# A two-block transformer kernel in fp32: gate and up of the second FFN by seven block products in place of eight

## The chip, the cores and the metric

One core of a Trainium2 chip (trn2) runs the whole program. The metric is device time in microseconds (us), median of several executions; lower is better.

## The reference, cut to what matters

Two layers are applied to 256 tokens of width 2048: a recurrent block with an FFN, then an attention block with an FFN. The change touches the second FFN alone:

```python
h2 = _rms(x, g_norm2) * (1 + sc2) + sh2          # 256 x 2048
gate, up = jnp.split(h2 @ w_ffn_in, 2, axis=-1)  # 2048 x 11264: gate | up, 5632 columns each
x = x + gt2 * ((jax.nn.silu(gate) * up) @ w_ffn_out)
```

All is float32. The kernel gets its precision from split products: each operand is a high part (rounded to float32r, the type of TensorE's fast pass) plus a low part (the rest, float32r too), and a product is high x high + low x high + high x low, three matmuls.

## The kernel before, in words

**Tiling.** Tokens are two blocks (tb) of 128. K = 2048 is 16 K-tiles of 128, in four groups (q) of 4. The FFN's 5632 columns are cut into 11 iterations of 512. In iteration i come gate (H times 512 columns), up (the same with the other half of the matrix), then the down product of the block of 512 hidden columns made one iteration earlier, over the four column blocks (n) of the output.

**Units and half-units.** Weights come in units of 1 MB (4 K-tiles x 512 columns), each a DMA that SP issues into one of four slots RAW0 to RAW3 (`load`, L363). `slot_free` makes SP wait until the unit four before is no longer read. A unit is two half-units (`sub`), each 2 K-tiles x 512 columns, 128x1024. For each, ScalarE writes the high part WHI (`hi`, L580), VectorE the low part WLO = RAW - WHI (`lo`, L1073), and TensorE multiplies (`sub` in the tensor block, kind "T", through `mm`, L1783): 2 K-tiles x 2 token blocks x 3 = 12 matmuls with 128 tokens stationary and 512 columns moving. An iteration has 24 half-units: 8 gate, 8 up, 8 down, 288 matmuls. Half-units are numbered through the whole program; the second FFN begins with number 552, its iteration 3 (the first that changes) with 616.

**Rings.** WHI and WLO have two places each, and in the FFNs a third (for the second FFN the three places are dealt out from half-unit 528 on, inside the output projection ahead of it). `ring(s)` gives a half-unit's place and how many half-units back the place was last used (deep); `hi` waits until TensorE is done with that one (semaphore `pe_sub`). Each engine works its queue strictly in order, and everything is ordered by semaphores: `hi_done` (ScalarE to VectorE), `lo_done` (VectorE to TensorE and SP), `free[pair]` (a PSUM pair is read out).

**PSUM.** The pairs A to D have two banks of 512 columns. Gate sums in A, up in B, down alternates between A and C. L724 (ScalarE) forms silu of A in G, L1302 (VectorE, `product`) multiplies by B, TensorE turns the result in 8 transposes (`hid_turn`, L2013), and L730 and L1307 write its high and low part, HID. `add_down(n)` (L1315, VectorE) adds a finished down block to YF and frees its pair; in the loop body it is placed behind low 20 and 22 for n = 0, 1, and behind low 0 and 2 of the next iteration for n = 2, 3.

**Modulation.** In the first three iterations VectorE also works on vectors of `w_ada_2`, which GpSimd loads (L514, 512 KB each, four slots); the last sum is `ada_bias` 24. Otherwise GpSimd computes nothing in this part. Just ahead of the FFN stands the boundary, where x is normalised and H formed (L1242 high part, L1243 low part).

**The loop.** Iterations 0 to 2 are written out, 3 to 8 are a loop on every engine, 9 and 10 are written out.

Of the kernel before, what the change touches and what calls it, by code (L numbers as in the profile page):

```python
# [22 lines left out]
T = 256  # L23
# [92 lines left out]
RING3 = ((2 * U_FFN1, 2 * U_WIN2 + 30), (2 * U_WOUT2 + 8, 2 * N_UNITS))  # L116


def ring(s):


    if s < 26:
        return s % 2, s
    for first, last in RING3:
        if first <= s < last:
            if s < first + 3:
                return (s - first) % 3, s - 47 if first == 2 * U_FFN1 else 2
            return (s - first) % 3, 3
    return s % 2, 2
# [25 lines left out]
class Counts:  # L155


    def __init__(self):
# [4 lines left out]
        self.quad, self.chain = Count(), Count()  # L163
        self.all = dict(unit=self.unit, sub=self.sub, A=self.A, B=self.B, C=self.C, ada=self.ada,
                        ada_group=self.ada_group, gate=self.gate, hid=self.hid, quad=self.quad, chain=self.chain)
# [25 lines left out]
def build(nc, x, c_rows, positions, rows_src, weights, ada_w, base_const, att_const, rg_a, rg_i, w_pool, out):  # L191
    w_in, w_out, w_gate, w_up, w_down, w_in2, w_uq, w_ukv, w_pa, w_pb, w_out2, w_ffin2, w_ffout2 = weights
    with ExitStack() as ctx:
# [18 lines left out]
        WLO2 = place("WLO2", [P, 2, COLS], F32R)  # L212
        here[0] = end
# [12 lines left out]
        WHI.append(WHI2)  # L226
        WLO.append(WLO2)
# [53 lines left out]
        chunk = lambda t, n: t[:, :, n * 512:(n + 1) * 512]  # L281
        row = lambda t, n: t[:, n * 512:(n + 1) * 512].rearrange("p (a b) -> p a b", a=1).to_broadcast([P, 2, 512])
# [10 lines left out]
        pe_tb = sem("pe_tb")  # L293
        free = {p: sem(f"free_{p}") for p in "ABC"}
# [52 lines left out]
        def _(sp):  # L347
            c = Counts()

            def slot_free():  # L350

                last = 2 * (c.unit.at - 4)
                if any(first <= last < end for first, end in NATIVE):
                    sp.wait_ge(pe_sub, last + 2)
                elif last >= 0:
# [23 lines left out]

            def ffn(k, wg, gcol, wu, ucol, wd):  # L380
# [7 lines left out]

                gate_up(0)
# [100 lines left out]

        def landed(eng, c):
# [7 lines left out]
        def _(pool):  # L499
# [56 lines left out]

            pool.wait_ge(free["B"], B_PROJ + 2)
            for g in (10, 11):
                ada(1, g * ADA_COLS)
# [3 lines left out]
        def _(act):  # L563
# [7 lines left out]
            def hi(n=1):  # L571

                for _ in range(n):
                    half, slot = c.sub.at % 2, c.unit.at % 4
# [142 lines left out]
            def ffn(k, skip, final=False):  # L717
# [15 lines left out]
                def body(skip=0, subs=24, previous=True, rows=False):  # L733
                    for s in range(skip, subs):
                        hi()
                        if s == 6 and previous:
# [5 lines left out]

                body(skip=skip, subs=16, previous=False)
                body()
                with act.Fori(2, NF - 2) as i:
                    c.enter(i - 2, unit=12, sub=24, hid=1, gate=1)
                    body()
                c.leave(NF - 4)
                body(rows=True)
# [309 lines left out]
        def _(dve):  # L1059
# [7 lines left out]
            def lo(n=1):  # L1067

                for _ in range(n):
                    half, slot = c.sub.at % 2, c.unit.at % 4  # L1070
# [1314 lines left out]
```

## Time and profile before

| | |
|---|---|
| time, median of 3 runs | 2519.57 us (2518.47 to 2519.95) |
| profiled execution: span from first to last instruction | 2517.7 us |
| profiled execution: time outside its span | not listed; the span is 1.9 us under the median of the runs |
| TensorE busy | 2440.5 us, 97% |
| VectorE busy | 1793.1 us, 71% |
| ScalarE busy | 1082.6 us, 43% |
| GpSimd busy | 223.2 us, 9% |
| DMA | 643 MB, mean 255 GB/s |

Busy time says how long an engine had an instruction running; matmuls overlap in the records, so TensorE's busy time is no measure of its peak. PE is TensorE, DVE VectorE, ACT ScalarE, POOL GpSimd, SP the engine that issues the weights' DMAs. "Idle before" is an engine's idle time just ahead of an instruction, with what ended it.

### The profile page before, as it was taken

What the parts mean: (1) busy time and instruction counts of PE and PEld (TensorE: products, weight loads), DVE (VectorE), ACT (ScalarE), POOL (GpSimd) and SP (SyncE); (2) the same over time, 40 slices, a digit from 0 to 9 for tenths busy, and PEclk for the clock granted to TensorE, in tenths of its full rate; (3) what the DMA queues carried; (4) which work ended last, traced back from release to release, by engine and by line L of the source; (5) the groups of instructions that cost most, each with busy time, mean ns of one, the idle gap of its engine ahead of it and who ended that gap; (6) DMA issues with size and microseconds to landing.
All of it is one profiled execution on the core that took longest, in us unless ns stands there. A gap on an engine that the chain in (4) does not pass through costs nothing.

```text
span 2517.7 us, 30560 instructions
## 1 busy us (share of the span) xinstructions
PE 2440.5 (97%) x11620; PEld 2000.9 (79%) x11620; DVE 1793.1 (71%) x1751; ACT 1082.6 (43%) x1243; POOL 223.2 (9%) x397
## 2 busy tenths in 40 slices
PE   4899999999999999999999999999999999999999
PEld 3679448888888888879997778788788888888887
DVE  6878887888888888778785445865688555555565
ACT  2035124444444444464346557644544444444443
POOL 4412210111111111001110000000011000000000
PEclk8899999999999999999999999999999999999999
DMA  9999996898889888647985555355588555555654
GB/s 367 382 337 354 403 358 225 308 328 313 312 321 328 317 318 323 209 152 279 341 291 162 166 172 161 117 184 200 198 320 285 191 192 185 197 184 192 208 184 150
DMA packets 291262, 643.01 MB, mean 255 GB/s; under 512 B 21883, under 2 KB 34749, under 8 KB 290269
## 3 DMA queue, kind: packets, MB, share of 16 engines
q1 hardware_dynamic: 234512, 436.45, 50.8%
q0 software_dynamic: 56096, 205.02, 21.8%
q8 instruction: 68, 1.11, 0.2%
q10 hardware_dynamic: 556, 0.18, 0.0%
q14 instruction: 30, 0.24, 0.0%
HBM read 639.47 MB, written 2.13 MB: 255 GB/s over the span
## 4 chain that ended last, share of the span: by engine, by line
PE 86%; DVE 5%; DMA 4%; ACT 4%; issue 1%; POOL 0%; DVEq 0%; ACTq 0%; POOLq 0%
PE PS L1783 84%; DMA R<-in_w_ada 3%; DVE R L1093 2%; ACT WHI L580 1%; DVE WLO L1073 1%; DMA RAW<-in_w_ffn_gate 1%; PE PS L2013 1%; PE PS L1907 1%; PE PS L1938 0%; DVE H L1243 0%; ACT R L658 0%; ACT L945 0%; ACT L588 0%; DVE H L1242 0%; ACT L937 0%
## 5 line engine op out<-in xcount | busy, mean ns | idle before, releaser
L1073 DVE TENSOR_TENSOR WLO<-RAW,WHI 128x1024 fp32r<-128x1024 f32 x760 | 929.7, 1225 | 610.3 <-ACT WHI L580 608.0
L580 ACT ACTIVATE WHI<-RAW 128x1024 fp32r<-128x1024 f32 x760 | 805.5, 1061 | 1118.3 <-PE PS L1783 1103.0
L1783 PE MATMUL PS<-WHI,H 128*128 128x512 f32 x4064 | 1263.1, 392 | 5.7 <-DVE WLO L1073 5.0
L1783 PEld LDWEIGHTS PS<-WHI,H 128*128 128x128 f32 x4064 | 755.0, 188 | 173.8 <-DVE WLO L1073 16.0
L1783 PE MATMUL PS<-WLO,H 128*128 128x512 f32 x2032 | 792.1, 390 | 0.0
L1783 PEld LDWEIGHTS PS<-WLO,H 128*128 128x128 f32 x2032 | 381.4, 188 | 80.8
L1093 DVE SCALAR_TENSOR_TENSOR R<-R,CA 128x1024 f32<-128x1024 f32 x326 | 417.6, 1281 | 36.7 <-DMA R<-in_w_ada 29.7
L1783 PE MATMUL PS<-WHI,HID 128*128 128x512 f32 x1280 | 395.2, 390 | 0.0
L514 POOL DMA_DIRECT2D R<-in_w_ada x284 | 150.9, 531 | 1586.7 <-DVE R L1090 555.1
L1783 PEld LDWEIGHTS PS<-WHI,HID 128*128 128x128 f32 x1280 | 239.3, 188 | 49.0
L1783 PE MATMUL PS<-WLO,HID 128*128 128x512 f32 x640 | 249.1, 389 | 0.0
L1783 PE MATMUL PS<-H,WHI 128*128 128x256 f32 x1120 | 204.8, 285 | 3.1 <-DVE WLO L1073 3.1
L1783 PEld LDWEIGHTS PS<-H,WHI 128*128 128x128 f32 x1120 | 174.7, 192 | 5.6 <-DVE WLO L1073 5.2
L1783 PE MATMUL PS<-H,WLO 128*128 128x256 f32 x560 | 158.4, 283 | 0.0
L1783 PEld LDWEIGHTS PS<-WLO,HID 128*128 128x128 f32 x640 | 120.1, 188 | 25.0
L1783 PE MATMUL PS<-RAW,YF 128*128 128x512 f32 x256 | 110.8, 592 | 0.0
L1783 PEld LDWEIGHTS PS<-H,WLO 128*128 128x128 f32 x560 | 107.3, 192 | 0.0
L1783 PEld LDWEIGHTS PS<-RAW,YF 128*128 128x128 f32 x256 | 48.2, 190 | 58.7 <-issue 58.7
L1315 DVE TENSOR_TENSOR YF<-PS,YF 128x1024 f32<-128x1024 f32 x72 | 87.7, 1218 | 0.0
L1783 PE MATMUL PS<-R,RAW 128*128 128x256 f32 x256 | 65.9, 425 | 13.3 <-ACT R L658 13.3
L1783 PEld LDWEIGHTS PS<-R,RAW 128*128 128x128 f32 x256 | 55.1, 217 | 22.8 <-ACT R L658 13.7
L1783 PE MATMUL PS<-R 128*128 128x256 f32 (+1 forms) x250 | 49.7, 341 | 3.7 <-ACT R L1031 1.8
(233 smaller groups left out, 1233.7 us busy)
## 6 DMA issues: line engine op xcount, KB each, us to landing
R<-in_w_ada POOLq DMA_DIRECT2D x348, 512.0 KB, 6.7
RAW<-in_w_in SPq DMA_DIRECT2D x88, 1024.0 KB, 5.6
RAW<-in_w_ffn_in SPq DMA_DIRECT2D x88, 1024.0 KB, 5.0
RAW<-in_w_ffn_gate SPq DMA_DIRECT2D x44, 1024.0 KB, 6.9
RAW<-in_w_ffn_up SPq DMA_DIRECT2D x44, 1024.0 KB, 5.3
RAW<-in_w_ffn_down SPq DMA_DIRECT2D x44, 1024.0 KB, 8.3
RAW<-in_w_ffn_out SPq DMA_DIRECT2D x44, 1024.0 KB, 5.0
RAW<-in_w_out SPq DMA_DIRECT2D x32, 1024.0 KB, 7.3
```

The lines of the kernel that those rows point to most:

```text
L514: pool.dma_start(ADA[slot], ada_w[layer][:, k, bass.ds(col, ADA_COLS)])\
L580: nc.scalar.activation(WHI[j][:, :, :], RAW[slot][:, 2 * half:2 * half + 2, :], ACT.Copy)\
L1073: nc.vector.tensor_tensor(WLO[j][:, :, :], RAW[slot][:, 2 * half:2 * half + 2, :], WHI[j][:, :, :].bitcast(F32), ALU.subtract).then_inc(lo ...
L1093: ins = nc.vector.scalar_tensor_tensor(acc, ADA[slot], scalar, acc, ALU.mult, ALU.add)
L1315: nc.vector.tensor_tensor(chunk(yt, n), PAIR[pair][:, :, :], chunk(yt, n), ALU.add)\
L1783: return nc.tensor.matmul(o, a, b, start=start, stop=stop, skip_group_check=True)
L1907: ins = nc.tensor.transpose(flat("D")[:, j * P:(j + 1) * P], acc[:, j * P:(j + 1) * P], ident)
L2013: ins = nc.tensor.transpose(four("B")[:, t, tb * P:(tb + 1) * P], G[:, tb * 512 + t * P:tb * 512 + (t + 1) * P], ident)
```

## The change

The second FFN's iterations 3 to 9 are called turns 0 to 6 and written out. In each, for the K-tile groups q = 0 and 1 (NS = 2), gate and up are taken together as one product of 2 x 2 blocks: the rows are the two token blocks, the columns gate and up, the inner index the two halves of the group (2 K-tiles each). Eight block products become seven, by sums and differences of blocks on both sides. Each of the seven pieces is a half-unit of its own with a WHI and a WLO, but only 6 matmuls (2 K-tiles x 3). Groups 2 and 3 keep their eight products, `both_halves`, 12 matmuls each. A turn has 30 half-units: 14 pieces (0 to 13), 4 gate (14 to 17), 4 up (18 to 21), 8 down (22 to 29).

- **Sums of weights**: four per group, 128x1024, on GpSimd (`column_sums`), in five places USUM in free parts of R.
- **Lows on GpSimd**: half-units 17, 21, 23 and 25 of each turn have their low part made by GpSimd (`low_here`); VectorE skips them.
- **Sums of H**: once, during iteration 0, GpSimd forms four combinations of H's blocks per group (`operand_sums`: one pass of 128x1024, four of 128x256) and their low parts (`operand_low`); ScalarE writes the high parts behind half-units 13 and 15 of iteration 0.
- **Ring**: four places in the turns, three again afterwards (`place_of`).
- **PSUM**: each pair's banks hold one of seven sums; ScalarE copies the shared first product (Q1_COPY), VectorE puts gate and up together in eight additions of 128x512 (`seven_ev`).
- **Hidden block**: turned in two halves (`half_turn`), each 128x512 for ScalarE and VectorE; `product` of iteration 2 comes forward to its half-unit 18.
- **Slots**: SP also waits for GpSimd's lows (`lo_pool`) and sums (`u_done`); order of a turn's loads: gate and up of group 0, of group 1, gate 2 and 3, up 2 and 3, four down.

```diff
-RING3 = ((2 * U_FFN1, 2 * U_WIN2 + 30), (2 * U_WOUT2 + 8, 2 * N_UNITS))
+NS = 2
+SEVEN_FIRST, SEVEN_LAST = 3, NF - 1
+U_SEVEN = U_FFN2 + 8 + 12 * 2
+SUB_SEVEN = 2 * U_SEVEN
+PER_SEVEN = 24 + 3 * NS
+GATE_END = 7 * NS + 2 * (4 - NS)
+UP_END = GATE_END + 2 * (4 - NS)
+POOL_LOW = (GATE_END - 1, UP_END - 1, UP_END + 1, UP_END + 3)
...
+def place_of(s):
+
+    if s < SUB_SEVEN:
+        return (s - RING3[1][0]) % 3
+    return (s - SUB_SEVEN) % 4 if s < SUB_AFTER else (s - SUB_AFTER) % 3
...
+    if s >= SUB_SEVEN:
+        before = [n for n in range(max(s - 8, RING3[1][0]), s) if place_of(n) == place_of(s)]
+        return place_of(s), s - before[-1] if before else 0
...
+            def column_sums(turn, q):
+
+                unit, first = U_SEVEN + 12 * turn + 2 * q, 4 * (NS * turn + q)
+                g, u = RAW[unit % 4], RAW[(unit + 1) % 4]
+                of = lambda n: USUM[(first + n) % 5]
+
+                def place_free(n):
+                    if first + n >= 5:
+                        t, m = divmod(first + n - 5, 4 * NS)
+                        sub = SUB_SEVEN + PER_SEVEN * t + m // 4 * 7 + 3 + m % 4
+                        pool.wait_ge(lo_done, dve_lows(sub + 1))
+                    else:
+                        pool.wait_ge(a_lo, NS)
+                        if first + n >= 2:
+                            pool.wait_ge(ada_bias, 24)
+
+                landed_unit(pool, unit)
+                landed_unit(pool, unit + 1)
+                place_free(0)
+                pool.tensor_tensor(of(0), g[:, 0:2, :], u[:, 0:2, :], ALU.add).then_inc(u_done, 1)
+                place_free(1)
+                pool.wait_ge(u_done, first + 1)
+                pool.tensor_tensor(of(1), of(0), u[:, 2:4, :], ALU.add).then_inc(u_done, 1)
+                place_free(2)
+                pool.tensor_tensor(of(2), u[:, 0:2, :], u[:, 2:4, :], ALU.add).then_inc(u_done, 1)
+                place_free(3)
+                pool.wait_ge(u_done, first + 2)
+                pool.tensor_tensor(of(3), of(1), g[:, 2:4, :], ALU.add).then_inc(u_done, 1)
...
+                        operand_low(NS - 1)
+            for turn in range(N_SEVEN):
+                for q in range(NS):
+                    column_sums(turn, q)
+                for at in POOL_LOW:
+                    unit, half = divmod(at - 7 * NS, 2)
+                    low_here(SUB_SEVEN + PER_SEVEN * turn + at, U_SEVEN + 12 * turn + 2 * NS + unit, half)
 
...
+                def high(src, ready, value):
...
+                    if deep:
+                        act.wait_ge(pe_sub, c.sub.value(1 - deep))
+                    else:
+                        act.wait_ge(ada_bias, 24)
+                    nc.scalar.activation(WHI[j][:, :, :], src, ACT.Copy).then_inc(hi_done, 1)
...
+                            if at == 11:
+                                act.wait_ge(half_t, turn + 1)
+                                nc.scalar.activation(HID[:, 0:2, 0:T], MISC.rearrange("p (a b) -> p a b", a=2), ACT.Copy)\
+                                    .then_inc(half_hi, 1)
+                            if at == 16:
+                                act.wait_ge(hid_t, c.hid.value(1))
+                                nc.scalar.activation(HID[:, 2:4, 0:T], MISC.rearrange("p (a b) -> p a b", a=2), ACT.Copy)\
+                                    .then_inc(hid_hi, 1)
+                                c.hid.at += 1
+                            if at == 7 * (NS - 1) + 4:
+                                act.wait_ge(pe_sub, first + 7 * (NS - 1) + 1)
+                                if turn:
+                                    act.wait_ge(seven_ev, 8 * turn)
+                                else:
+                                    act.wait_ge(a_lo, NS)
+                                nc.scalar.activation(Q1_COPY, bank("A", 0), ACT.Copy).then_inc(q1_copied, 1)
+                            if at == GATE_END + 5:
+                                act.wait_ge(seven_ev, 8 * turn + 6)
+                                nc.scalar.activation(G, G, ACT.Silu).then_inc(gate_done, 1)
+                                c.gate.at += 1
...
+                            if at in (1, 3):
+                                add_down(2 + at // 2, 4)
+                            if at == 11:
+                                dve.wait_ge(half_hi, turn + 1)
+                                nc.vector.tensor_tensor(HID[:, 0:2, T:2 * T], half, HID[:, 0:2, 0:T].bitcast(F32),
+                                                        ALU.subtract).then_inc(half_lo, 1)
+                            if at == 16:
+                                dve.wait_ge(hid_hi, c.hid.value(1))
+                                nc.vector.tensor_tensor(HID[:, 2:4, T:2 * T], half, HID[:, 2:4, 0:T].bitcast(F32),
+                                                        ALU.subtract).then_inc(hid_lo, 1)
+                                c.hid.at += 1
+                            if at == 7 * NS + 1:
+                                dve.wait_ge(q1_copied, turn + 1)
+                                dve.wait_ge(pe_sub, first + last + 5)
+                                if turn == 0:
+                                    dve.wait_ge(a_lo, NS)
+                                nc.vector.tensor_tensor(vy_sum, bank("C", 0), Q1_COPY, ALU.subtract).then_inc(seven_ev, 1)
+                            if at == 7 * NS + 2:
+                                dve.wait_ge(pe_sub, first + last + 6)
+                                dve.wait_ge(seven_ev, 8 * turn + 1)
+                                nc.vector.tensor_tensor(X_SUM, bank("C", 1), vy_sum, ALU.add).then_inc(seven_ev, 1)
+                                nc.vector.tensor_tensor(w_sum, bank("B", 1), vy_sum, ALU.add).then_inc(seven_ev, 1)
+                                dve.wait_ge(seven_ev, 8 * turn + 3)
+                                nc.vector.tensor_tensor(vy_sum, bank("B", 1), X_SUM, ALU.add).then_inc(seven_ev, 1)
+                            if at == GATE_END + 3:
+                                dve.wait_ge(pe_sub, first + GATE_END)
...
+                                nc.vector.tensor_tensor(silu[:, 0, :], bank("A", 1), Q1_COPY, ALU.add).then_inc(seven_ev, 1)
+                                nc.vector.tensor_tensor(silu[:, 1, :], bank("D", 0), X_SUM, ALU.subtract).then_inc(seven_ev, 1)
+                            if at == UP_END + 3:
+                                dve.wait_ge(pe_sub, first + UP_END)
+                                dve.wait_ge(seven_ev, 8 * turn + 4)
+                                nc.vector.tensor_tensor(w_sum, bank("B", 0), w_sum, ALU.add).then_inc(seven_ev, 1)
+                                nc.vector.tensor_tensor(vy_sum, bank("D", 1), vy_sum, ALU.add).then_inc(seven_ev, 1)
+                            if at == UP_END + 4:
+                                dve.wait_ge(gate_done, c.hid.value(1))
+                                dve.wait_ge(seven_ev, 8 * turn + 8)
+                                nc.vector.tensor_tensor(G, WY_SUM, G, ALU.mult).then_inc(up_done, 1)
+                            if at in (UP_END + 5, UP_END + 7):
+                                add_down((at - UP_END - 5) // 2, 4)
...
+                def piece(out_, high, low, first, last):
+
+                    j, _ = ring(c.sub.at)
+                    low_ready()
+                    for k in range(2):
+                        mm(out_, high(k), WHI[j][:, k, :], first and k == 0)
+                        mm(out_, low(k), WHI[j][:, k, :], False)
+                        ins = mm(out_, high(k), WLO[j][:, k, :], False, last and k == 1)
+                    ins.then_inc(pe_sub, 1)
+                    c.sub.at += 1
...
+                def by_sevens(turn):
+
+                    ev = 8 * (turn - 1)
+                    if turn == 0:
+                        pe.wait_ge(a_lo, NS)
+                    for q in range(NS):
+                        first, last = q == 0, q == NS - 1
+                        plain = lambda at, tb: [lambda k, x=x: H[:, at + k, x + tb * P:x + (tb + 1) * P] for x in (0, T)]
+                        mixed = lambda m: [lambda k, of=of: of[q][:, m, k, :] for of in (AHI, ALO)]
+                        if first:
+                            pe.wait_ge(free["A"], c.A.value())
+                        piece(bank("A", 0), *plain(4 * q, 0), first, last)
+                        piece(bank("A", 1), *plain(4 * q + 2, 0), first, False)
+                        if first:
+                            if turn:
+                                pe.wait_ge(seven_ev, ev + 7)
+                            else:
+                                pe.wait_ge(up_done, c.hid.value(1))
+                        piece(bank("B", 0), *mixed(3), first, False)
+                        piece(bank("B", 1), *mixed(0), first, last)
+                        if q == 0 and turn == 0:
+                            row_turn(k, gate_at, 24)
+                        if first:
+                            pe.wait_ge(free["C"], c.C.value())
+                        piece(bank("C", 0), *mixed(1), first, last)
+                        if q == 1:
+                            pe.wait_ge(half_lo, turn + 1)
+                            half_turn(1)
+                        piece(bank("C", 1), *mixed(2), first, last)
+                        if first:
+                            if turn:
+                                pe.wait_ge(seven_ev, ev + 6)
+                            else:
+                                pe.wait_ge(ada_bias, 24)
+                        piece(bank("D", 0), *plain(4 * q + 2, 1), first, False)
+                        if q == 0:
+                            if turn:
+                                pe.wait_ge(seven_ev, ev + 8)
+                            else:
+                                pe.wait_ge(row_ev, k + 1)
+                            pe.wait_ge(up_done, c.hid.value(1))
+                            half_turn(0)
+                    for q in range(NS, 4):
+                        for half in range(2):
+                            both_halves(bank("A", 1), bank("D", 0), 4 * q + 2 * half, False, q == 3 and half == 1)
+                    pe.wait_ge(hid_lo, c.hid.value(1))
+                    for q in range(NS, 4):
+                        for half in range(2):
+                            both_halves(bank("B", 0), bank("D", 1), 4 * q + 2 * half, q == NS and half == 0,
+                                        q == 3 and half == 1)
+                    c.gate.at += 1
+                    pe.wait_ge(q1_copied, turn + 1)
+                    pe.wait_ge(seven_ev, 8 * turn + 5)
+                    for n in range(4):
+                        group("AC"[n % 2], kind="T", src=HID, units=1)
+                    c.hid.at += 1
+
                 previous = {3: hid_turn}
                 gate(turned=(k, "DC"))
```

## Rows read from the trace of the kernel before

**Rows 1.** Page, part 1: busy us (share of span), instructions.

```profile
PE 2440.5 (97%) x11620; PEld 2000.9 (79%) x11620; DVE 1793.1 (71%) x1751; ACT 1082.6 (43%) x1243; POOL 223.2 (9%) x397
```

**Rows 2.** Chain that ended last, second FFN: start us, us, what.

```profile
2039.40 65.31 PE PS L1783 x288
2104.70 0.87 PE PS L2013 x8
2105.58 65.33 PE PS L1783 x288
...
2171.78 65.30 PE PS L1783 x288
```

**Rows 3.** Busy time by stretch, the seven iterations: busy us (instructions).

```profile
1961.40:2027.60 66.20, 66.20 (x298) 54.88 (x297) 36.22 (x31) 27.29 (x26) 0.00 (x0) 1.00 0.57 191
1961.40:2424.80 463.40, 463.40 (x2075) 384.09 (x2074) 253.52 (x211) 191.20 (x183) 0.00 (x0) 1.00 0.58 193
```

**Rows 4.** Who waited for whom, 1961.4 to 2424.8 us: total, times, longest.

```profile
ACT WHI L580 <- PE PS L1783: 260.7, 161, 2.0
DVE WLO L1073 <- ACT WHI L580: 209.9, 168, 2.4
```

**Rows 5.** Groups by line, 2000 to 2400 us: busy, mean ns, idle before.

```profile
L1073 DVE TENSOR_TENSOR WLO<-RAW,WHI 128x1024 fp32r<-128x1024 f32 x146 | 179.0, 1226 | 182.9 <-ACT WHI L580 182.9
L1315 DVE TENSOR_TENSOR YF<-PS,YF 128x1024 f32<-128x1024 f32 x24 | 29.2, 1218 | 0.0
...
L580 ACT ACTIVATE WHI<-RAW 128x1024 fp32r<-128x1024 f32 x145 | 153.8, 1061 | 225.2 <-PE PS L1783 225.2
...
L730 ACT ACTIVATE HID<-PS 128x1024 fp32r<-128x1024 f32 x6 | 6.1, 1010 | 0.0
```

**Rows 6.** Timeline of VectorE: start us, us of one or several (xcount).

```profile
1774.60 0.69 DVE L1189 TENSOR_TENSOR R<-PS,R 128x512 f32<-128x512 f32 x1
...
1798.10 2.35 DVE L1073 TENSOR_TENSOR WLO<-RAW,WHI 128x1024 fp32r<-128x1024 f32 x2
...
2161.15 1.23 DVE L1073 TENSOR_TENSOR WLO<-RAW,WHI 128x1024 fp32r<-128x1024 f32 x1 [0.36 <-ACT WHI L580]
2162.30 1.22 DVE L1315 TENSOR_TENSOR YF<-PS,YF 128x1024 f32<-128x1024 f32 x1
```

**Rows 7.** Timeline around one hand-over: TensorE, ScalarE, VectorE.

```profile
2167.79 0.39 PE L1783 MATMUL PS<-WLO,H 128*128 128x512 f32 x1
...
2168.22 1.06 ACT L580 ACTIVATE WHI<-RAW 128x1024 fp32r<-128x1024 f32 x1 [1.66 <-PE PS L1783]
...
2169.31 1.23 DVE L1073 TENSOR_TENSOR WLO<-RAW,WHI 128x1024 fp32r<-128x1024 f32 x1 [1.49 <-ACT WHI L580]
```

**Rows 8.** DMA issues, 1990 to 2440 us: size, median us to landing.

```profile
RAW<-in_w_ffn_in SPq DMA_DIRECT2D x55, 1024.0 KB, 5.0
RAW<-in_w_ffn_out SPq DMA_DIRECT2D x27, 1024.0 KB, 5.0
```

**Rows 9.** Timeline of GpSimd and VectorE, 114 to 117 us.

```profile
114.75 1.82 POOL L537 MEMSET R<- 128x2048 f32 x1
...
114.58 1.28 DVE L1093 SCALAR_TENSOR_TENSOR R<-R,CA 128x1024 f32<-128x1024 f32 x1 [0.83 <-DMA R<-in_w_ada]
116.70 1.28 DVE L1093 SCALAR_TENSOR_TENSOR R<-R,CA 128x1024 f32<-128x1024 f32 x1 [0.83 <-DMA R<-in_w_ada]
```

**Rows 10.** Timeline at the start of the second FFN, VectorE and GpSimd.

```profile
1797.49 0.69 DVE L1243 TENSOR_TENSOR H<-R,H 128x512 fp32r<-128x512 f32 x1
...
1775.58 2.15 POOL L514 DMA_DIRECT2D R<-in_w_ada  x4 [472.61 <-DVE R L1189]
1833.27 0.53 POOL L514 DMA_DIRECT2D R<-in_w_ada  x1 [55.54 <-DVE R L1090]
```

More of the change, by code:

```diff
@@ L489, in build, with landed_unit, seven_source @@
         EXTRA = {U_KPE: 1, **{U_LAT + n: 3 for n in range(7)}}
+        def landed_unit(eng, n):
+            extra = sum(v for u, v in EXTRA.items() if u % 4 == n % 4 and u <= n)
+            eng.wait_ge(raw_in[n % 4], 16 * (n // 4 + 1 + extra))
+        def seven_source(turn, q, e):
+            unit = U_SEVEN + 12 * turn + 2 * q
+            g, u = RAW[unit % 4], RAW[(unit + 1) % 4]
+            return (g[:, 0:2, :], g[:, 2:4, :], u[:, 2:4, :])[e] if e < 3 else USUM[(4 * (NS * turn + q) + e - 3) % 5]
         def landed(eng, c):
@@ L557, in _, with low_here @@
+            def low_here(sub, unit, half):
+                j, _ = ring(sub)
+                pool.wait_ge(hi_done, sub + 1 - native_before(sub))
+                pool.tensor_tensor(WLO[j][:, :, :], RAW[unit % 4][:, 2 * half:2 * half + 2, :],
+                                   WHI[j][:, :, :].bitcast(F32), ALU.subtract).then_inc(lo_pool, 1)
             pool.wait_ge(free["B"], B_PROJ + 2)
             for g in (10, 11):
-                ada(1, g * ADA_COLS)
+                for k in range(KT):
+                    pool.wait_ge(ada_op, c.ada.value(-3))
+                    pool.dma_start(ADA[c.ada.at % 4], ada_w[1][:, k, g * ADA_COLS:(g + 1) * ADA_COLS])\
+                        .then_inc(ada_in[c.ada.at % 4], 16)
+                    c.ada.at += 1
+                    if g == 10 and k == 3:
+                        pool.wait_ge(x_step, 12)
+                        for q in range(NS):
+                            operand_sums(q)
+                            if q:
+                                operand_low(q - 1)
+                        operand_low(NS - 1)
@@ L1350, in body @@
                             lo()
+                        if s == 18 and early:
+                            product(3)
                         if s == 1 and up:
@@ new lines, in half_turn, with both_halves @@
+                def half_turn(n):
+                    for t in (2 * n, 2 * n + 1):
+                        for tb in range(2):
+                            ins = nc.tensor.transpose(MISC[:, t % 2 * T + tb * P:t % 2 * T + (tb + 1) * P],
+                                                      G[:, tb * 512 + t * P:tb * 512 + (t + 1) * P], ident)
+                    ins.then_inc(hid_t if n else half_t, 1)
+                def both_halves(one, two, at, first, last):
+                    j, _ = ring(c.sub.at)
+                    low_ready()
+                    for k in range(2):
+                        for tb, out_ in ((0, one), (1, two)):
+                            high, low = (H[:, at + k, x + tb * P:x + (tb + 1) * P] for x in (0, T))
+                            mm(out_, high, WHI[j][:, k, :], first and tb == 1 and k == 0)
+                            mm(out_, low, WHI[j][:, k, :], False)
+                            ins = mm(out_, high, WLO[j][:, k, :], False, last and k == 1)
+                    ins.then_inc(pe_sub, 1)
+                    c.sub.at += 1
@@ L2307, in _ @@
             ffn(3, False, mod_at(1, 5))
[L2308 removed]
+            assert c.sub.at == N_SUBS
 def kernel(**inputs):
```

234 lines of the change are left out of this document (202 added, 32 removed).

## The prediction

> **What bounds the kernel now.** I read the page's shares first, then the chain that ended last, then the stretch that the change rewrites, then single instructions. TensorE is busy 97% of the span; VectorE, the next, 71%, and GpSimd 9% [rows 1]. In the second FFN the chain is TensorE alone: 288 matmuls in 65.3 us, then the 8 transposes of the hidden block in 0.87 us, over and over [rows 2]. So an iteration takes 66.2 us and one 128x512 matmul 65.31 / 288 = 0.2268 us of the stream (the 390 ns of its row overlap with the next). The seven iterations that change run from 1961.4 to 2424.8 us: 463.4 us, TensorE 100% busy at a granted clock of 1.00 (the 2.4 GHz level), VectorE busy 253.5 us (55%), ScalarE 191, GpSimd 0, the DMA engines 0.58 [rows 3]. ScalarE and VectorE mostly wait for TensorE to give back a ring place [rows 4]. Only fewer matmuls shorten this stretch, and only if the operands still come in time.
>
> **What goes.** Gate and up of one group of four K-tiles are 4 half-units of 12 matmuls, 48. By sevens they are 7 pieces of 6, 42. Two groups save 12 matmuls an iteration: 12 x 0.2268 = 2.72 us, in seven iterations 19.05 us. The columns, types and transposes stay. All of it lies on the chain.
>
> **What the pieces ask of the other engines.** 14 pieces of 6 x 0.2268 = 1.361 us make a window of 19.05 us per iteration. Each piece needs its own high part on ScalarE (1.06 us) and low part on VectorE (1.23 us) [rows 5]; back to back VectorE starts one every 1.13 to 1.15 us, and an addition out of PSUM takes the same 1.15 [rows 6]. In the window VectorE has 14 lows (16.1 us), two additions of the down product (2.3) and half a hidden block (0.6, from 0.69 for 128x512 [rows 6]): 19.0 of 19.05 us. ScalarE has 14 x 1.06 and two copies of half width, 15.9. It fits, with nothing to spare. What carries it is the ring, now four deep: TensorE's half-unit ends at 2168.18, the high part starts 2168.22, the low starts 2169.31 and ends 2170.54 [rows 7], a round of 2.4 us (2.56 from the start of TensorE's next piece, since its last matmul ends 0.16 us into it); TensorE comes to that place three pieces, 4.08 us, later. Slack 1.5 us; an addition of 1.15 goes into it. I take no stall here. Outside the window VectorE has 12 lows, nine passes of half width out of PSUM, two additions and a product, some 23 us in 44.4: covered. The other waits (the halves of the hidden block, the copied first product, the bank sums) each sit one to three pieces behind their producers, where the ring has them ready; I cost them at nothing, and they are due next if VectorE falls back. The loop is written out; its back edges cost nothing measurable now (65.30 to 65.33 us each time [rows 2]), so this is zero too.
>
> **The two joints.** Here I find a cost. The old ring has three places, counted from another start: half-unit 615 lies in place (615-528) mod 3 = 0, and the first piece, 616, is given place 0 as well. Its high part must wait until the half-unit just before it is multiplied. Behind it stand in VectorE's queue low 0, low 1 and the addition that frees pair A, for which the first piece waits. So TensorE stands for 0.16 + 2.4 + 1.15 + 1.15 = 4.9 us, once. The pieces after that find VectorE 1.15 us per low against 1.361: no more. On leaving, the first half-unit is only two deep and again waits for low 0 and one addition: 0.16 + 2.4 + 1.15 - 2.72 = 1.0 us. Together 5.9 us.
>
> **DMA and slots.** The bytes are the same, 12 units of 1 MB per iteration, 5.0 us from issue to landing [rows 8]. Slots of the two groups are freed by GpSimd's sums now. The up unit of the first group is loaded when low 25 is done, some 18 us before the window, and lands 12 us before it; that of the second follows low 29 and lands about 3 us before it. SP only waits at its own slots. Nothing lost.
>
> **GpSimd, the unknown.** Per iteration it gets 8 column sums and 4 lows of 128x1024, 12 passes, and no row shows it doing arithmetic on two inputs. The nearest is a memset of 128x2048 in 1.82 us [rows 9]: 0.91 us for 1024 elements of one stream, the lower bound; three streams (two read, one written) one after the other give 2.73, the upper. Two reads one after the other with the write hidden give 1.8. I take 2.3, the middle of 1.8 and 2.73. By a row of the Trainium skill ("GPSIMD Engine Reference", 3.1) an fp32 tensor_tensor of 2048 elements takes 4497 ns, thus an estimate of 2.25 here; no run here shows it, and the sum would not change. In time: eight sums at 2.3 need 18.4 us from 12 us before the window, so they end some 6 us into it, and the last is wanted at 14.5. At 2.73 it is 10: still in time. So GpSimd's own speed does not bind; what it does to VectorE may. Bounds for that: nothing (the VectorE pass with two SBUF inputs that began 0.17 us ahead of the memset kept its 1.28 us, and the memset ran beside it [rows 9], though a memset only writes), and full exclusion, rival one. I take nothing to slight, because the nearest row shows none. A gain is excluded: nothing gets shorter from a second user.
>
> **Before the first turn** GpSimd forms the mixed operands of H: ten passes and two lows, at most 18 us, after H is finished at 1798.2. Its queue has the next load of w_ada behind them, which goes out at 1833.3 [rows 10]: 17 us to spare. ScalarE's two copies stand behind half-units 13 and 15, where it idles 1.66 us ahead of each high part [rows 7]. Nothing.
>
> **Sum.** -19.05 + 5.9 = -13.15 us, on a span of 2517.7 us, which stands 1.9 us under the median of 2519.57; I subtract from the median: 2506.4 us.
>
> **Rivals.**
> One, **VectorE and GpSimd exclude each other**: a VectorE pass with two SBUF inputs (every low) and a GpSimd pass that reads SBUF cannot run together. The four sums of the second group fall into the window, as its unit lands 3 us ahead of it. Then lows and sums share one path: 16.1 + 4p against 19.05 + 1.5 of slack, a stall of 4p - 4.45; with p = 2.3, 4.75 us, against 2.72 saved. That is +2.03 x 7 = 14.2, with the joints +20.1: 2539.7 us, slower. It decides from p = 1.6 on (a stall of 1.9 leaves 0.84 us a turn, and seven of those pay the joints); p = 1.8 gives 2525.7, p = 2.73 2552. For it: VectorE's window is full, so whatever GpSimd takes is added. Against: no row of before shows it, and rows 9 show none for a write. The Trainium skill ("SBUF — State Buffer", Who interferes with whom) states just such a rule, that a Vector instruction with two SBUF inputs contends with a GpSimd instruction that reads SBUF and that the second one fully blocks; nothing in this trace can show or deny it for a read. By that rule the time is this rival's.
> Two, **a mild mutual slowing**: lows overlapping a sum are stretched. Up to some 1.5 us per window goes into the slack; at 3 us, 1.5 us a turn is lost: 7 x (1.5 - 2.72) + 5.9 = -2.6, 2517 us, no change.
> Three, **the joints are covered** after all: -19.05, 2500.5 us, if the first piece does not wait as I read it.
>
> **How the numbers follow.** The forecast (no or slight interference) 0.50, with its own range of 2500 to 2512; full exclusion 0.36; the middle case 0.12, spread over all three signs; something else 0.02. A difference of about 0.2%, 5 us, is what a measurement here can tell from none. Faster 0.54, same 0.07, slower 0.39. The range reaches from the joints nearly covered (2502) to exclusion at slightly over my p (2541); about 2 in 10 stay out, most of it above.
>
> **What would show it.** Right: TensorE's busy runs in the seven turns sum to 63.5 us each, one gap of about 5 us near 1961 us, low rows of VectorE unchanged at 1.23 us, GpSimd passes near 2.3 us. Wrong: lows of 2 us and more, or gaps ahead of them, wherever a GpSimd pass runs; TensorE waiting for VectorE's lows around pieces 4, 11 and 12 of every turn; or GpSimd passes above 3 us, with ScalarE waiting for a sum.

## The result, and the profile after

The changed kernel takes 2553.2 us (median; 2552.23 to 2554.75), the kernel before 2519.57: ratio 1.0133, with a 95% interval of 1.0119 to 1.0148. It is slower by 33.6 us; I had forecast 13 us less. The profiled execution has a span of 2552.1 us, 34.4 more than before. Executions of one kernel agree within 0.5% here; one of the four of experiment 5 took 6018.29 us and is left out of its time. The page's first part, to hold against [rows 1]:

```profile
PE 2432.2 (95%) x11536; PEld 1982.8 (78%) x11536; DVE 1931.9 (76%) x1828; ACT 1130.1 (44%) x1301; POOL 483.5 (19%) x493
```

The 84 matmuls are gone (11620 to 11536). TensorE's busy time falls by 8.3 us only, not by 19: beside a stop the records of two matmuls no longer overlap, and behind the first stop the matmuls are slower. VectorE has 138.8 us more busy time for 77 more instructions, GpSimd 260 us more. Next the chain that ended last, where [rows 2] had TensorE alone; one turn, from one transpose of the half block to the next, and the way out of the seven turns (start us, us, what):

```profile
2130.09 0.44 PE PS L2399 x4
2130.53 32.69 PE PS L2123 x144
2163.30 1.07 ACT WHI L949
2164.39 6.17 DVE WLO L1622 x2
2170.56 1.14 DVE YF L1585
2171.70 5.54 DVE WLO L1622 x2
2177.24 1.14 DVE YF L1585
2178.37 3.33 DVE WLO L1622 x2
2181.70 1.13 DVE YF L1585
2182.84 10.24 DVE WLO L1622 x4
2193.12 7.10 PE PS L2123 x30
2200.22 0.44 PE PS L2399 x4
...
2457.65 1.15 DVE YF L1585
2458.93 11.13 PE PS L2123 x48
```

From 2164.4 to 2193.1 the chain is VectorE: ten lows in 25.28 us and three additions in 3.41. The additions, which read PSUM, keep the 1.15 us of before; a low goes at 2.5 us instead of 1.15. The same pattern stands six times, at each passage from one turn to the next; the first turn has a stop of its own. The turn takes 2200.22 - 2130.09 = 70.1 us, 66.2 before [rows 2]. The stretches (PE, PEld, DVE, ACT, POOL busy with instructions; granted clock, DMA share, GB/s), against [rows 3]:

```profile
1961.90:1982.70 20.80, 12.42 (x48) 9.50 (x47) 18.63 (x11) 11.47 (x12) 12.77 (x5) 0.84 0.29 102
2122.97:2193.12 70.15, 64.89 (x284) 52.30 (x284) 56.01 (x42) 33.89 (x34) 34.26 (x12) 1.00 0.53 180
```

The first row is the way into the turns, at a mean granted clock of 0.84. In a turn (second row) TensorE's records cover 64.89 of 70.15 us. The clock is full, so this is waiting. The groups by line and shape, 2100 to 2400 us (busy, mean ns, idle before), against [rows 5]:

```profile
L1622 DVE TENSOR_TENSOR WLO<-RAW,WHI 128x1024 fp32r<-128x1024 f32 x76 | 139.3, 1854 | 53.7 <-ACT WHI L949 53.7
...
L1622 DVE TENSOR_TENSOR WLO<-R,WHI 128x1024 fp32r<-128x1024 f32 x36 | 59.8, 1699 | 0.0
...
L739 POOL TENSOR_TENSOR WLO<-RAW,WHI 128x1024 fp32r<-128x1024 f32 x16 | 38.4, 2402 | 108.7 <-ACT WHI L949 108.7
...
L733 POOL TENSOR_TENSOR R<-R,RAW 128x1024 f32<-128x1024 f32 x10 | 33.7, 3374 | 0.0
...
L1585 DVE TENSOR_TENSOR YF<-PS,YF 128x1024 f32<-128x1024 f32 x19 | 23.0, 1213 | 0.0
```

VectorE's low goes from 1226 ns to 1854 (and 1699 for those that read a sum). The same kind of pass on GpSimd takes 2402 ns where it stands beside no low of VectorE (L739) and 2760 to 3374 in the four sums (L733 is the last). L1585 is unchanged at 1213 against 1218. Where the long ones lie, the timelines of the same turn say; VectorE first, then GpSimd:

```profile
2164.39 6.17 DVE L1622 TENSOR_TENSOR WLO<-RAW,WHI 128x1024 fp32r<-128x1024 f32 x2 [0.42 <-ACT WHI L949]
2170.49 1.21 DVE L1585 TENSOR_TENSOR YF<-PS,YF 128x1024 f32<-128x1024 f32 x1
...
2195.26 2.35 DVE L1622 TENSOR_TENSOR WLO<-R,WHI 128x1024 fp32r<-128x1024 f32 x2
```

```profile
2163.74 2.40 POOL L725 TENSOR_TENSOR R<-RAW,RAW 128x1024 f32<-128x1024 f32 x1 [5.13 <-issue]
...
2169.44 3.36 POOL L730 TENSOR_TENSOR R<-RAW 128x1024 f32<-128x1024 f32 x1
...
2188.62 3.37 POOL L733 TENSOR_TENSOR R<-R,RAW 128x1024 f32<-128x1024 f32 x1
2204.72 2.40 POOL L739 TENSOR_TENSOR WLO<-RAW,WHI 128x1024 fp32r<-128x1024 f32 x1 [12.73 <-ACT WHI L949]
```

The first slow pair of lows begins 0.65 us after the first sum; once the eighth sum has ended at 2191.99 a pair takes 2.35 us again. GpSimd's 3.36 us is about one pass of its own (2.40, of which some hides) and one low (1.13). Both fit engines that wait for each other's whole pass, turn about. An addition from PSUM at 2170.49 lies beside the sum of 2169.44 and keeps its 1.21 us.

**Where 34.4 us come from**, by the starts of matmuls in TensorE's timeline (the next one would begin 0.23 us after the last). The matmul after iteration 2 would have begun at about 1961.75 (1961.27 before). The first piece begins at 1968.88: 7.1 us. The first matmul behind the seven turns would have begun at 2457.80 and begins at 2458.93: 1.1 us. Between lie 488.9 us; the turns without a wait are 63.53 us each (measured in the second experiment), 444.7, so 44.2 us are waits and lower clock inside the turns: 40.2 in the six passages, the rest in the first turn. Saved are 7 x (66.20 - 63.53) = 18.7. Sum: 0.5 + 7.1 + 1.1 + 44.2 - 18.7 = 34.2.

### The profile page after: what moved, and what is told of

The parts are those of the page before. It is cut to its first block, busy times and chain, and to the rows that moved or that the text cites. A ratio compares the mean times of both kernels' runs of the same rounds, so it can differ in the third digit from the quotient of the medians.

```text
span 2552.1 us, 30121 instructions
## 1 busy us (share of the span) xinstructions
PE 2432.2 (95%) x11536; PEld 1982.8 (78%) x11536; DVE 1931.9 (76%) x1828; ACT 1130.1 (44%) x1301; POOL 483.5 (19%) x493
## 4 chain that ended last, share of the span: by engine, by line
PE 76%; DVE 13%; DMA 5%; ACT 3%; issue 1%; POOL 0%; DVEq 0%; ACTq 0%; POOLq 0%
PE PS L2123 74%; DVE WLO L1622 6%; DMA R<-in_w_ada 5%; DVE R L1363 2%; ACT WHI L782 1%; DVE WLO L1343 1%; DVE YF L1585 1%; DMA RAW<-in_w_ffn_gate 1%; PE PS L2257 1%; PE PS L2363 1%; PE PS L2288 0%; ACT WHI L949 0%; DVE H L1513 0%; ACT L1215 0%; ACT L790 0%
## 5 line engine op out<-in xcount | busy, mean ns | idle before, releaser
L2123 PE MATMUL PS<-WHI,H 128*128 128x512 f32 x3784 | 1180.1, 393 | 37.1 <-DVE WLO L1622 17.0
L1343 DVE TENSOR_TENSOR WLO<-RAW,WHI 128x1024 fp32r<-128x1024 f32 x592 | 730.8, 1237 | 395.5 <-ACT WHI L782 393.1
L782 ACT ACTIVATE WHI<-RAW 128x1024 fp32r<-128x1024 f32 x592 | 627.2, 1061 | 862.5 <-PE PS L2123 845.1
L2123 PEld LDWEIGHTS PS<-WHI,H 128*128 128x128 f32 x3784 | 702.2, 188 | 201.4 <-issue 24.9
L2123 PE MATMUL PS<-WLO,H 128*128 128x512 f32 x1892 | 738.3, 390 | 0.0
L2123 PEld LDWEIGHTS PS<-WLO,H 128*128 128x128 f32 x1892 | 355.5, 188 | 75.8
L1622 DVE TENSOR_TENSOR WLO<-RAW,WHI 128x1024 fp32r<-128x1024 f32 x126 | 217.7, 1749 | 100.1 <-ACT WHI L949 100.1
L949 ACT ACTIVATE WHI<-RAW 128x1024 fp32r<-128x1024 f32 x154 | 163.1, 1061 | 199.5 <-PE PS L2123 199.5
L739 POOL TENSOR_TENSOR WLO<-RAW,WHI 128x1024 fp32r<-128x1024 f32 x28 | 67.3, 2403 | 190.1 <-ACT WHI L949 190.1
```

What stands on the lines that cost most here:

```text
L739: pool.tensor_tensor(WLO[j][:, :, :], RAW[unit % 4][:, 2 * half:2 * half + 2, :], WHI[j][:, :, :].bitcast(F32), ALU.subtract).then_inc(lo_ ...
L782: nc.scalar.activation(WHI[j][:, :, :], RAW[slot][:, 2 * half:2 * half + 2, :], ACT.Copy)\
L949: nc.scalar.activation(WHI[j][:, :, :], src, ACT.Copy).then_inc(hi_done, 1)
L1343: nc.vector.tensor_tensor(WLO[j][:, :, :], RAW[slot][:, 2 * half:2 * half + 2, :], WHI[j][:, :, :].bitcast(F32), ALU.subtract).then_inc(lo ...
L1622: nc.vector.tensor_tensor(WLO[j][:, :, :], src, WHI[j][:, :, :].bitcast(F32), ALU.subtract)\
L2123: return nc.tensor.matmul(o, a, b, start=start, stop=stop, skip_group_check=True)
```

## The experiments

Theory A in the expectations is mutual exclusion, the prediction's first rival: VectorE passes with both inputs in SBUF and GpSimd passes that read SBUF run one at a time. Its rivals are named where they stand. In experiments 1 to 4 the kernel before took 2520.83 us (2518.43 to 2522.83), in 5 to 8 2519.23 (2517.79 to 2521.65); ratios are against those.

**1. The joints alone.** The ring places of the turns are counted one further, so that the first piece does not share its place with the half-unit just before it; the wait on leaving the turns goes with the same edit.

```diff
-    return (s - SUB_SEVEN) % 4 if s < SUB_AFTER else (s - SUB_AFTER) % 3
+    return (s - SUB_SEVEN + 1) % 4 if s < SUB_AFTER else (s - SUB_AFTER) % 3
```

> The changed kernel with the ring's places shifted by one in the turns, so that the first piece and the half-unit before it do not share a place; nothing else. Theory A (VectorE passes with two SBUF inputs and GpSimd passes that read SBUF exclude each other): the one wait of about 7 us ahead of the first piece and the 1 us wait on leaving go, but turn 0 then shows the same 6.7 us of waits as the others; each turn stays at 70.1 us; 2546 us (2543 to 2549). Rival B (the joints are the main cost, since a stop of 7 us also lowers TensorE's granted clock): below 2535 us.

Measured: 2551.38 us (2551.15 to 2554.35), ratio 1.0125 [1.0108, 1.0142]; span 2549.7. The later turns still take 70.1 us (the half turn's transposes start at 2059 and 2129). The first turn's 7.1 us stop has shrunk to 2.4 us (again with a lower clock behind it) and the one on leaving is gone, but the first turn now has stops like the others', as its chain shows:

```profile
1964.55 5.49 DVE WLO L1622 x2
1971.17 10.24 DVE WLO L1622 x4
1981.45 7.10 PE PS L2123 x30
```

So the joints are 2.4 us of the span and no more while the sums are there: in the first turn the same queue of lows stood behind. The time lies above the expected range of 2543 to 2549 us: I had taken the whole stop for gone, and 2.4 us of it stayed. Rival B is out: the loss is not the joints'.

**2. No sums.** Pieces 3 to 6 of each group take raw blocks in place of the sums, GpSimd has no lows, and slots are freed after the group's last low. The eight sums per turn are left out; the matmuls, highs and lows are all there (the lows all on VectorE).

```diff
-POOL_LOW = (GATE_END - 1, UP_END - 1, UP_END + 1, UP_END + 3)
+POOL_LOW = ()
...
-            return (g[:, 0:2, :], g[:, 2:4, :], u[:, 2:4, :])[e] if e < 3 else USUM[(4 * (NS * turn + q) + e - 3) % 5]
+            return (g[:, 0:2, :], g[:, 2:4, :], u[:, 2:4, :], g[:, 0:2, :], g[:, 2:4, :], u[:, 0:2, :],
+                    u[:, 2:4, :])[e]
...
-                for q in range(NS):
-                    column_sums(turn, q)
```

> The changed kernel without GpSimd in the turns: the eight column sums are left out (pieces 3 to 6 take blocks of the raw weights in their place) and the four lows go back to VectorE. Left out: the sums of weights. Theory A: every low is back at 1.23 us, turns take 63.5 us, only the joints are left: 2507 us (2505 to 2510). Rival C (VectorE and ScalarE have too much to do for pieces of 1.36 us, GpSimd or not): turns stay above 66.2 us, 2520 us or more.

Measured: 2510.09 us (2509.67 to 2511.11), at the upper edge of the expected range; ratio 0.9961 [0.9946, 0.9975]; span 2507.8. The chain at the joint and in a turn, a group by line (2000 to 2400 us), and two stretches:

```profile
1962.62 2.36 DVE WLO L1619 x2
...
1966.22 8.03 PE PS L2120 x24
...
1985.78 0.44 PE PS L2396 x4
1986.21 55.81 PE PS L2120 x246
```

```profile
L1619 DVE TENSOR_TENSOR WLO<-RAW,WHI 128x1024 fp32r<-128x1024 f32 x187 | 225.3, 1223 | 101.6 <-ACT WHI L946 100.0
```

```profile
1966.22:1974.25 8.03, 8.03 (x26) 6.31 (x27) 5.99 (x6) 3.19 (x3) 0.00 (x0) 0.69 0.00 0
1985.78:2049.30 63.52, 63.52 (x286) 52.60 (x285) 47.68 (x46) 33.92 (x34) 0.00 (x0) 1.00 0.58 199
```

Every wait inside the turns is gone, with more work on VectorE than in the changed kernel (30 lows a turn, not 26). A turn is 63.52 us: the window's 19.0 us of VectorE in 19.05 does fit, and so do the ring, the halves of the hidden block and the slots. The first joint costs its stop, 4.9 us by the starts of matmuls (4.78 idle), and then lower clock: 24 matmuls take 8.03 us at a mean granted clock of 0.69, against 5.73 us at full clock in experiment 5. On leaving, the stop is 1.1 us.

**3. Writes only.** Each sum becomes three memsets of the same size at the same place in GpSimd's queue, with the same waits and signals; GpSimd has no lows. The sums' values are left out. The cut shows the first of the four sums of a group; the others are changed alike.

```diff
-                pool.tensor_tensor(of(0), g[:, 0:2, :], u[:, 0:2, :], ALU.add).then_inc(u_done, 1)
+                step(pool.memset(of(0), 0.0))
+                step(pool.memset(of(0), 0.5))
+                pool.memset(of(0), 0.25).then_inc(u_done, 1)
```

> As the run without GpSimd lows, but each column sum is replaced by three memsets of the same place (some 2.8 us together, no SBUF read), with the same waits and signals. Left out: the sums of weights, constants stand in their places. Theory A (only a GpSimd pass that reads SBUF excludes VectorE): lows stay at 1.23 us and turns at 63.5 us, 2507 us (2505 to 2512). Rival D (GpSimd's sums come too late, whatever VectorE does): turns about as long as with the sums, over 2540 us. Rival E (any GpSimd pass, writes too, takes the port): lows of 2 us and more, over 2535 us.

Measured: 2510.51 us (2509.38 to 2512.78), ratio 0.9962 [0.9947, 0.9976]. GpSimd and VectorE in one window:

```profile
2163.01 0.96 POOL L730 MEMSET R<- 128x1024 f32 x1 [1.75 <-DVE WLO L1630]
2164.02 0.96 POOL L731 MEMSET R<- 128x1024 f32 x1
```

```profile
2164.00 3.49 DVE L1630 TENSOR_TENSOR WLO<-R,WHI 128x1024 fp32r<-128x1024 f32 x3
```

GpSimd is busy nearly as long (2.9 us for a sum), writes three times the bytes, and the waits of its sums remain; three lows take 3.49 us, as without it, and a turn is 63.52 us, 22.7 of them with GpSimd busy. So neither GpSimd's writes, nor the waits for its sums, nor the freeing of slots by them cost anything. What costs is what a sum has and a memset lacks: it reads two inputs from SBUF. (It also adds, which this run does not part from the reading.) This is also why [rows 9] misled me: they show a memset.

**4. No lows on GpSimd**, the sums kept: only `POOL_LOW = ()`.

> The changed kernel with the four lows of a turn back on VectorE, the eight sums still on GpSimd. Theory A: the four lows lie outside the stretch where TensorE waits, and low 25, which frees the slot of the first group's up unit, takes 1.1 us in place of 2.4; so the sums begin about 1.3 us earlier and at most that is won per turn: 2548 us (2543 to 2554). Rival C (VectorE is overloaded): four more passes of 1.13 us a turn, 2565 to 2585 us.

Measured: 2547.68 us (2546.05 to 2549.34), ratio 1.0107 [1.009, 1.0124]; the turn 69.2 us. VectorE takes on four lows a turn and the span is 6.0 us shorter (2546.1 against 2552.1): a low moved to GpSimd was no relief. The loss stays with the sums; their groups read 2938, 2805, 3352 and 3382 ns, about as in the changed kernel. The last of them, 2000 to 2400 us:

```profile
L733 POOL TENSOR_TENSOR R<-R,RAW 128x1024 f32<-128x1024 f32 x12 | 40.6, 3382 | 0.0
```

This run and experiment 3 differ in nothing but the passes that stand for the sums, additions here and memsets there: 2547.68 against 2510.51 us, a turn of 69.2 against 63.5. It is the pair that isolates the cause.

**5. Neither sums nor the joint**: experiment 2 with the edit of 1.

> As the run without sums, with the ring's places shifted so that neither joint shares a place. Left out: the sums of weights. Theory A: nothing but the saved matmuls remains: 2501 us (2499 to 2504), 9 us below the run without sums, of which some 5.9 us is the waiting itself and the rest the lower granted clock after it. Rival: the joints are cheap when nothing else is late: 2507 us or more.

Measured: 2503.39 us (2500.63 to 2503.71, three executions), ratio 0.9932 [0.9912, 0.9952]; span 2501.6.

```profile
1962.73 0.87 issue
1963.60 5.73 PE PS L2120 x24
```

Against experiment 2 that is 6.2 us of span for the two joints alone. The stop falls to 0.87 us, the one on leaving is gone, and the next 24 matmuls take 5.73 us instead of 8.03, at full clock. This is about the floor of the scheme as it is ordered here.

**6. The sums on VectorE.** The whole computation; all sums but the first four of the first turn move into VectorE's queue, after half-units 1, 3, 6, 10 (second group) and 27 to 29 and 0 (next turn's first group); no lows on GpSimd; the joint as in 1.

```diff
+                SUM_AFTER = (1, 3, 6, 10)
+                NEXT_AFTER = (27, 28, 29, 30)
...
+                    nc.vector.tensor_tensor(of(n), a, b, ALU.add).then_inc(u_dve, 1)
```

> The computation of the changed kernel, complete, with the column sums and all lows on VectorE (sums of the next turn's first group behind lows 27, 28, 29 and 0, those of the second behind lows 1, 3, 6 and 10) and the joints mended. GpSimd only makes the first four sums. Theory A: no exclusion any more, a sum costs 1.15 us and not 2.4; the window now holds 16.1 + 5.7 + 2.9 us of VectorE's work in 19.05 us, so some 1.5 to 2 us of waiting per turn against 2.72 saved: 2512 us (2507 to 2518). Rival C (VectorE cannot carry it): 2525 us or more.

Measured: 2515.8 us (2513.06 to 2521.53), ratio 0.999 [0.9981, 1.0], hardly told apart from the kernel before; span 2512.6. Chain, and one group of 2000 to 2400 us:

```profile
1960.16 5.61 issue
1965.78 8.09 PE PS L2161 x24
```

```profile
L1656 DVE TENSOR_TENSOR R<-R,RAW 128x1024 f32<-128x1024 f32 x24 | 29.3, 1220 | 0.2
```

VectorE does in 1.22 us what GpSimd did in 2.4 to 3.4, and from the first piece on no low is longer than 1.23. The turn falls from 70.1 us (69.2 in experiment 4, which also has every low on VectorE) to 64.6, though VectorE has all 30 lows and all eight sums. What is left is the full window, as counted (1.1 us a turn), and a stop of 5.6 us in the first turn. That stop is this run's own: VectorE's first sum waits, idle for 2.33 us, until GpSimd has ended the fourth of the sums left to it, and the addition that frees pair A stands behind.

**7. The sums on VectorE, the two groups apart.** As 6 (the cut is against 6), but the turn's order is group 0's pieces, the four gate half-units of groups 2 and 3, group 1's pieces, the rest; loads, slots and waits follow.

```diff
+ORDER = [*range(7), *range(14, 18), *range(7, 14), *range(18, 30)]
...
-                SUM_AFTER = (1, 3, 6, 10)
+                SUM_AFTER = (7, 8, 9, 10)
```

> As the run with sums on VectorE, and the turn is reordered: the seven pieces of group 0, the four gate half-units of groups 2 and 3, the seven pieces of group 1, then up and down; the sums of group 1 lie behind the four gate half-units. VectorE then has 10.4 us in 9.5, 9.2 in 10.9, 8.7 in 9.5, 9.4 in 10.9 and 18.6 in 21.8. Theory A: every stretch fits, turns of 63.5 us: 2501 us (2499 to 2506). Rival C: over 2510 us.

Measured: 2506.19 us (2504.99 to 2509.79), at the upper edge of the expected range; ratio 0.9947 [0.9931, 0.9964]: faster than both kernels, by 13 us than the one before and some 47 than the changed one. Its turns have no wait; VectorE is busy 56.0 us in 63.5:

```profile
1966.21 2.03 issue
1968.24 7.29 PE PS L2168 x24
...
1991.58 51.73 PE PS L2168 x228
2043.31 0.44 PE PS L2444 x4
```

```profile
1991.58:2055.10 63.52, 63.52 (x285) 52.58 (x285) 56.01 (x53) 34.15 (x35) 0.00 (x0) 1.00 0.57 197
```

It keeps one stop of 2.03 us in the first turn and the lower clock after it (7.29 us for 24 matmuls). The profiled execution is the slowest of the four.

**8. The same order, the sums on GpSimd.** The rival to 6 and 7 was that the order alone gives the gain, since the sums then fall where VectorE has room. This run has the order, loads and slots of 7, with all eight sums on GpSimd as in experiment 4.

> The same reordered turn with the eight sums back on GpSimd, lows on VectorE. Theory A: in a turn 30 lows of 1.14 and 8 sums of 2.4 exclude each other, 53.4 us of 63.5, so it can fit on the whole, but four sums that alternate with lows need some 13 us, more than the 10.9 us of the gate half-units: some waiting ahead of the pieces of group 1, none ahead of group 0; 2510 us (2502 to 2525). Rival F (how the work is spread is all that matters, not which engine sums): as the reordered turn with sums on VectorE, 2501 us.

Measured: 2522.57 us (2514.29 to 2525.02), ratio 1.001 [1.0, 1.0019], again hardly told apart from the kernel before; the turn 66.5 us. The groups, 2000 to 2400 us, of this run:

```profile
L1628 DVE TENSOR_TENSOR WLO<-RAW,WHI 128x1024 fp32r<-128x1024 f32 x133 | 241.9, 1843 | 30.1 <-ACT WHI L954 28.1
L1628 DVE TENSOR_TENSOR WLO<-R,WHI 128x1024 fp32r<-128x1024 f32 x48 | 58.0, 1221 | 3.6 <-ACT WHI L954 3.1
```

The lows of pieces 3 to 6, which no longer lie beside a sum, are back at 1221 ns, the others stand at 1843 in the mean. TensorE waits most where the four gate half-units are, whose lows alternate with sums (four lows in 13.2 us), but also 0.8 us ahead of group 0, where I had expected nothing. The order helps, as a turn falls from 69.2 us (experiment 4) to 66.5, but the engine matters as much: from 66.5 to 63.5 with the sums on VectorE, 16 us of the median in all. So rival F is out, and GpSimd as a helper is worse here than no helper.

## Why the prediction was wrong

**What bounds the kernel, and what goes: right.** TensorE's stream bounds it, and a turn without waits is 63.52 us. The saving is 18.7 us, against 19.05 by my terms.

**The window: right, and no help.** I had VectorE at 19.0 of 19.05 us and the ring with 1.5 us of slack, and took no stall. Experiment 2 has exactly that load and no stall. But a window that is full to the last half microsecond turns every microsecond taken from VectorE into one of TensorE's, and I said so only in the rival's part.

**The joints: the stops right, the clock left out.** I had 4.9 + 1.0 us. Without the sums the stops measured 4.9 and 1.1 (experiment 2); what I left out is the 2.3 us that the lower clock cost after the first (24 matmuls in 8.03 us, not 5.73). With the sums the first stop was 7.1 us, as two lows in it took 4.55 us in place of 2.36. In the changed kernel itself the joints were worth only 2.4 us (experiment 1), since other waits stood behind them.

**DMA and slots: right.** Waiting for the signals of GpSimd's sums costs nothing (experiment 3).

**GpSimd's own speed: right.** I took 2.3 us for a pass; alone it takes 2.40. The estimate from the Trainium skill's figure ("GPSIMD Engine Reference", 3.1), halved to 2.25, stands 0.15 under it.

**GpSimd beside VectorE: the step that failed.** "I take nothing to slight, because the nearest row shows none." The row [rows 9] was a write beside a pass with two inputs; what the change adds are passes that read two inputs. The row was the nearest one, but it lacked the very property in dispute, so it was no evidence between the two bounds. I set the term at 0; it measured 44.3 us, the span of the changed kernel above that of experiment 2. Experiments 2 to 4 and 6 put the loss there: without the reads, or with the reads on VectorE, lows are 1.22 us; with them 1.7 to 1.9 in the mean. I gave this rival 0.36 though no row spoke against it. The rule of the Trainium skill ("SBUF — State Buffer", Who interferes with whom), that a two-input Vector pass and a GpSimd pass that reads SBUF contend, by an exclusive lock, is what the timelines show: lows of up to 3.4 us beside sums.

**Rival one: the right mechanism, its price too low.** I worked out a stall of 4.75 us a turn, 2539.7 us in all. A turn in the middle loses 70.16 - 63.53 = 6.6 us, the mean of the seven is 44.2 / 7 = 6.3. I let only the four sums of the second group fall into the window, as if the others would cost VectorE nothing. In fact the eight run from 2163.7 to 2192.0, with only two pauses (2.30 and 1.16 us, for a place that a low must free), and alternate with lows from the start, 15 us ahead of the window's first piece at 2178.43. Six of the eight take 3.2 to 3.4 us beside lows, the other two 2.4. VectorE comes into the window late, and TensorE's waits lie elsewhere than I had put them: at half-unit 28 and at pieces 0, 4, 6 and 7, and none near 11 and 12:

```profile
2171.84 0.70 PE L2123 MATMUL PS<-WHI,HID 128*128 128x512 f32 x2 [0.48 <-DVE YF L1585]
...
2185.42 0.47 PE L2123 MATMUL PS<-WHI,AHI 128*128 128x512 f32 x1 [1.26 <-DVE WLO L1622]
```

(TensorE's timeline of the same turn in the changed kernel; in brackets the idle time and who ended it.) The loss needs no lateness of the sums: no wait of ScalarE for a sum stands among the waits of the turns. That my formula gives 2552 us, nearly the measured time, at p = 2.73 is chance: at the measured 2.40 it gives 2542.5.

**Before the first turn: right in effect.** GpSimd's sums of H lie beside VectorE's lows there too and take from 1798.45 to 1824.08, 25.6 us and not my 18, still ahead of the next load at 1833.7. TensorE's stream comes 0.5 us later to the first turn than before. In experiment 2, which forms the sums of H too but no sums of weights, it comes no later (1961.28 against 1961.27), so the sums of H cost nothing. The 0.5 us may be the spread between executions: with sums of weights the moment lies at 1960.0 in experiment 6 and at 1962.4 in experiment 8.

**The sum.** By my own steps, with the sizes of experiment 2: -18.7 + 4.9 + 1.1 and 2.3 for the clock is -10.4; its span stands 9.9 us under before. So without the sums I would have been some 3 us off, for the clock above all. The other 44.3 us, to the changed kernel's 34.4 over before, are the term that I set at zero: the waits in the turns, and 2.2 us by which the first stop is longer. That experiment 7 lands on my 2506.4 us is chance, since it is another kernel.

**Open.** Whether GpSimd passes with one input would exclude VectorE as well was not tried, nor were VectorE passes with one input in SBUF. The kernel of experiment 7 with a cheaper way into the turns was not built either.

## What to carry to other kernels

Before work goes to GpSimd, list which VectorE passes will run beside it: if they have two inputs in SBUF and GpSimd's pass reads SBUF, count the sum of both, each at its own length, as one queue, and not as two engines (here lows of 1.13 us and sums of 2.40). Half the speed on a shared path was a loss here, whatever the busy shares said: VectorE did all the extra work itself, with 7.5 us a turn to spare, once the two tight groups stood apart. And a row is evidence for an unknown cost only if it has the property in dispute; where it lacks it, keep the bounds open.

## What the runs showed of the hardware

- **Exclusion pass by pass.** GpSimd's two-input 128x1024 pass takes 2.40 us alone and 3.2 to 3.4 beside a row of lows; a VectorE low 1.23 alone, 2.2 to 3.4 beside it. It goes by whole passes, also for short ones: GpSimd's 128x256 pass ahead of the first turn takes 0.74 us alone and 1.60 beside lows.

```profile
1803.45 1.60 POOL L695 TENSOR_TENSOR R<-R 128x256 f32<-128x256 f32 x1
...
1806.81 0.74 POOL L697 TENSOR_TENSOR R<-R 128x256 f32<-128x256 f32 x1
```

  By these rows more and shorter passes on GpSimd would be no way out; in the turns this was not tried.
- **What is not touched:** VectorE passes with one input in PSUM (1213 ns beside sums), and VectorE's lows beside GpSimd's memsets (0.96 us each).
- **The clock after a stop.** The granted clock (1.00 is the 2.4 GHz level; a mean below it mixes in the 1.2 GHz level) was 0.69 over the 8 us after 4.8 us of idle time (experiment 2), 0.64 over the 5 us after 7.0 us (the changed kernel), and 1.00 after 0.87 us (experiment 5). The stops of 0.4 to 1.5 us inside the turns left it at 1.00. Near 2 us the length alone does not settle it: 2.03 us (experiment 7) were followed by 0.77 over 7.3 us, 2.04 us (experiment 8) by 1.00.
